# Feed-forward gate and up tiles as Strassen block products, weight-quarter sums on GpSimd (POOL)

## What is computed

```python
def swiglu_ffn(x, w_in, w_out):
    gate, up = jnp.split(x @ w_in, 2, axis=-1)
    return (jax.nn.silu(gate) * up) @ w_out

for i in range(DEPTH):                       # DEPTH = 2
    x = x + 0.5 * swiglu_ffn(rmsnorm(x, norm_g[i, 0]), ffn_w_in[i, 0], ffn_w_out[i, 0])
    ...
    x = x + 0.5 * swiglu_ffn(rmsnorm(x, norm_g[i, 2]), ffn_w_in[i, 1], ffn_w_out[i, 1])
```

## Time and profile before

| | |
|---|---|
| median of three runs | 2656.32 us |
| span of the profiled execution (the page gives no other time of it) | 2655.9 us |
| PE busy | 2612.3 us, 98% |
| DVE busy | 1569.0 us, 59% |
| ACT busy | 1004.4 us, 38% |
| POOL busy | 365.6 us, 14% |
| DMA | 238.23 MB, 90 GB/s on average |

### The profile page before, as it was taken

The page is one execution under the profiler, slowest core; times in us unless marked ns, Lnnn a source line. Parts: engine busy times, 40 slices in busy tenths (PEclk is TensorE's granted clock), DMA queues, the critical chain, the costliest instruction groups (busy, mean ns, idle before and its releaser), DMA issues.

```text
span 2655.9 us, 37310 instructions
## 1 busy us (share of the span) xinstructions
PE 2612.3 (98%) x14575; PEld 2099.3 (79%) x14575; DVE 1569.0 (59%) x2288; ACT 1004.4 (38%) x1423; POOL 365.6 (14%) x334
## 2 busy tenths in 40 slices
PE   7999999999999989999999999999999999999999
PEld 5787878787777768888888888888888864888887
DVE  6656655676767664444465444554444798644445
ACT  4544445446666642222252222232222313422223
POOL 1110101012000011111121111121111421211110
PEclk8999999999999999999999999999999999999999
DMA  3222222122222112333212223223222362233221
GB/s 117 82 80 81 80 65 95 34 80 88 79 82 78 69 53 91 98 103 99 95 64 95 96 100 101 97 94 97 95 95 95 113 170 73 97 100 101 97 95 63
DMA packets 171509, 238.23 MB, mean 90 GB/s; under 512 B 6513, under 2 KB 149371, under 8 KB 171411
## 3 DMA queue, kind: packets, MB, share of 16 engines
q1 hardware_dynamic: 163523, 217.23, 25.0%
q0 software_dynamic: 6080, 19.43, 2.6%
q10 hardware_dynamic: 1808, 0.21, 0.1%
HBM read 232.36 MB, written 4.40 MB: 89 GB/s over the span
## 4 chain that ended last, share of the span: by engine, by line
PE 88%; DVE 7%; ACT 2%; issue 1%; DMA 1%; POOL 0%; ACTq 0%; DVEq 0%; SPq 0%; POOLq 0%
PE ps L389 20%; PE ps L391 20%; PE ps L390 20%; PE ps L813 5%; PE ps L815 4%; PE ps L814 4%; DVE w_lo L366 1%; DVE dw_y L2283 1%; DVE probs L1756 1%; PE ps L375 1%; PE ps L377 1%; PE ps L376 1%; PE ps L1596 1%; PE ps L1607 1%; ACT w_hi L361 1%
## 5 line engine op out<-in xcount | busy, mean ns | idle before, releaser
L361 ACT ACTIVATE w_hi<-w_raw 128x2048 fp32r<-128x2048 f32 x203 | 388.4, 1914 | 894.8 <-PE ps L391 889.4
L389 PE MATMUL ps<-h_hi,w_hi 128*128 128x512 f32 x1456 | 569.2, 391 | 0.0
L391 PE MATMUL ps<-h_hi,w_lo 128*128 128x512 f32 x1456 | 568.0, 390 | 0.0
L390 PE MATMUL ps<-h_lo,w_hi 128*128 128x512 f32 x1456 | 567.8, 390 | 0.0
L366 DVE TENSOR_TENSOR w_lo<-w_raw,w_hi 128x2048 fp32r<-128x2048 f32 x203 | 464.9, 2290 | 126.7 <-ACT w_hi L361 126.6
L434 DVE SCALAR_TENSOR_TENSOR xT<-ps,xT 128x512 f32<-128x512 f32 x488 | 325.1, 687 | 132.5 <-PE ps L391 131.9
L389 PE MATMUL ps<-a_hi,w_hi 128*128 128x512 f32 x976 | 380.4, 390 | 2.6 <-issue 2.6
L390 PE MATMUL ps<-a_lo,w_hi 128*128 128x512 f32 x976 | 380.2, 390 | 0.0
L391 PE MATMUL ps<-a_hi,w_lo 128*128 128x512 f32 x976 | 380.2, 390 | 0.0
L1843 POOL TENSOR_TENSOR f_gate<-f_gate,n_rstd 128x512 f32<-128x512 f32 x88 | 176.8, 2011 | 1126.5 <-ACT f_gate L1837 1126.5
L389 PEld LDWEIGHTS ps<-h_hi,w_hi 128*128 128x128 f32 x1456 | 273.8, 188 | 58.1 <-issue 1.7
(11 more groups left out here) (369 smaller groups left out, 2928.5 us busy)
## 6 DMA issues: line engine op xcount, KB each, us to landing
w_raw<-in_ffn_w_in_dram SPq DMA_DIRECT2D x88, 1024.0 KB, 5.0
w_raw<-in_ffn_w_out_dram SPq DMA_DIRECT2D x44, 1024.0 KB, 4.9
w_raw<-in_a_w_in_dram SPq DMA_DIRECT2D x24, 1024.0 KB, 5.3
w_raw<-in_b_w_in_dram SPq DMA_DIRECT2D x16, 1024.0 KB, 5.4
w_raw<-in_conv_w_pw_dram SPq DMA_DIRECT2D x12, 1024.0 KB, 5.7
shifted<-glu_scratch POOLq DMA_DIRECT2D x32, 264.0 KB, 7.8
w_raw<-in_a_w_out_dram SPq DMA_DIRECT2D x8, 1024.0 KB, 4.9
w_raw<-in_b_w_out_dram SPq DMA_DIRECT2D x8, 1024.0 KB, 4.9
```

What stands on the lines that cost most here:

```text
L361: nc.scalar.activation(w_hi[:, t % 2], w_raw[:, t % 2], ACT.Copy).then_inc(hi_done, 1)
L389: nc.tensor.matmul(dst, wh, xh, start=(k == 0), stop=False)
L390: nc.tensor.matmul(dst, wh, xl, start=False, stop=False)
L391: m = nc.tensor.matmul(dst, wl, xh, start=False, stop=last)
```

## The change

In steps 2 to 10 of each feed-forward layer (`PLAIN` = 2 steps stay as they were) a gate or up tile is multiplied as 2x2 blocks: hidden channels in two halves of 128, input channels in two halves of 4 x 128, tokens in two halves of 256 (`HT`). The tile has four weight quarters of 128x512 (`corner`). Seven block products (numbered 1, 2, 5, 6, 7, 3, 4, Winograd's form) replace eight; each has 4 x 3 matmuls of 256 columns. Products add up in PSUM: 6, 7 and 4 go into the bank of 1, and 3 into that of 5, after ACT has copied what was there.

- POOL makes four sums of weight quarters per tile (`gp_step`), two of them over the raw tile. The two multiplications by `n_rstd` of such a step are gone: `n_rstd` now goes into the input blocks.
- ACT rounds (`act_mix`) and DVE subtracts (`dve_mix`) seven 128x512 parts per tile in place of one of 128x2048. They lie in `wg`, `wu` and one of the two buffers of `w_hi` and `w_lo`; the output tile of these steps has only the other one (`weight_slot`), so its rounding waits for the last output chunk of the step before (`mix_out_round`).
- Once per layer, in steps 0 and 1, DVE makes the scaled input `hs_a`, `hs_b` (8 instructions), POOL four sums of its halves (128x1024), ACT and DVE split the seven input blocks into `mix_early` and `mix_late` (`act_hs`, `dve_hs`).
- Eight small recombinations and products of 256 columns per step on DVE, five copies on ACT. In what follows g6 is product 6 of the gate tile and u6 that of the up tile; p1g, p5g, u2g (p1u, p5u, u2u) are ACT's copies of sums in PSUM, c11g, c12g, c22g (c11u, ...) DVE's recombinations of a quarter of gate or up, t2, t3, t4 POOL's input sums.
- `f_gate` moves onto `n_h`. The pooling stage's `band` now shares space with the new buffers: POOL writes it to DRAM during the attention stage and reads it back after the first feed-forward layer.
- The loops over the steps are written out.

The core of the diff (PE's products and order, POOL's sums, then the start of a steady step on ACT and DVE and the layer's start on DVE):

```diff
+            elif x in (6, 7):
+                mix_act.wait(pe, f"{'p1' if x == 6 else 'u2'}{u}", i)
+            elif x == 3:
+                mix_act.wait(pe, f"p5{u}", i)
+            elif x == 4:
+                mix_dve.wait(pe, f"c22{u}", i)
+            elif name in ("u2", "u5"):
+                mix_dve.wait(pe, "c11g" if name == "u2" else "c11u", i)
+            wh, wl = mix_slot(f, u, x)
...
+            for k in range(4):
+                ins = mm(wh, 0, first and k == 0, False)
+                mm(wh, 1, False, False)
+                ins = mm(wl, 0, False, k == 3)
+            mix_pe.done(name, ins)
 
         def pe_ff(pe, f, m, q):
...
+            for s in range(1, PLAIN):
+                for u in "guo":
+                    pe_tile(pe, step_tile(f, s, u))
+            for s in range(PLAIN, FF_STEPS):
+                for u, x in (("g", 1), ("g", 2), ("g", 5), ("g", 6), ("u", 1), ("u", 2), ("g", 7), ("u", 6), ("u", 5),
+                             ("g", 3), ("g", 4), ("u", 7)):
+                    pe_mix(pe, f, s, u, x)
+                to = step_tile(f, s, "o")
+                pe.wait_ge(lo_done, to + 1 + SPLIT_CREDIT)
+                pe.wait_ge(pair_ready, pairs_before(to) + 1)
+                pe_out(pe, to, range(0, 3))
+                pe_mix(pe, f, s, "u", 3)
+                pe_mix(pe, f, s, "u", 4)
+                pe_out(pe, to, range(3, 8))
             pe_tile(pe, t + 2 + 3 * (FF_STEPS - 1))
...
+        def gp_step(pool, f, s, u):
+
+            tt, t, i = nc.gpsimd.tensor_tensor, step_tile(f, s, u), step_at(f, s)
+            pool.wait_ge(raw_loaded[t % 2], 16 * (t // 2 + 1))
+            mix_lo_before(pool, i, u, 2)
+            tt(mix_s1, corner(t, 1, 0), corner(t, 1, 1), ALU.add).then_inc(mix_sums[u], 1)
+            mix_lo_before(pool, i, u, 3)
+            pool.wait_ge(mix_sums[u], 4 * i + 1)
+            tt(mix_s2, mix_s1, corner(t, 0, 0), ALU.subtract).then_inc(mix_sums[u], 1)
+            tt(corner(t, 1, 0), corner(t, 0, 0), corner(t, 1, 0), ALU.subtract).then_inc(mix_sums[u], 1)
+            pool.wait_ge(mix_lo[u], 6 * i + 2)
+            pool.wait_ge(mix_sums[u], 4 * i + 2)
+            tt(corner(t, 0, 1), corner(t, 0, 1), mix_s2, ALU.subtract).then_inc(mix_sums[u], 1)
+
+        def gp_ff(pool, f):
+            tt = nc.gpsimd.tensor_tensor
+            left, right = slice(0, HT), slice(HT, T)
             for c in range(2):
-                pool.wait_ge(f_silu, f_count(f, s, c, i))
-                nc.gpsimd.tensor_tensor(f_gate[:, c], f_gate[:, c], n_rstd[:], ALU.mult).then_inc(f_gated, 1)
-
-        def gp_ff(pool, f):
-            gp_gated(pool, f, 0)
-            with pool.Fori(0, FF_STEPS // 2) as i:
-                for r in range(2):
-                    gp_gated(pool, f, 1 + r, i)
-
-        def ff_round(act, f, t, i=None):
+                gp_gated(pool, f, 0, c)
+            pool.wait_ge(hs_made, 8 * f + 8)
+            tt(mix_t3[:], hs_b[:, :, right], hs_a[:, :, right], ALU.subtract).then_inc(hs_summed, 1)
+            pool.wait_ge(hs_summed, 4 * f + 1)
+            tt(hs_a[:, :, right], hs_a[:, :, right], hs_a[:, :, left], ALU.subtract).then_inc(hs_summed, 1)
+            gp_gated(pool, f, 1, 0)
+            pool.wait_ge(hs_summed, 4 * f + 2)
+            tt(mix_t2[:], hs_b[:, :, right], hs_a[:, :, right], ALU.subtract).then_inc(hs_summed, 1)
+            gp_gated(pool, f, 1, 1)
+            pool.wait_ge(hs_summed, 4 * f + 3)
+            tt(mix_t4, hs_b[:, :, left], mix_t2[:], ALU.subtract).then_inc(hs_summed, 1)
+            for s in range(PLAIN, FF_STEPS):
+                gp_step(pool, f, s, "g")
+                gp_step(pool, f, s, "u")
...
+        def act_step(act, f, s):
...
+
+            first = s == PLAIN
+            if not first:
+                mix_out_round(act, f, s)
+            pe_done("g1")
+            m("p1g", fn(f_gate[:, 0, 0:HT], half_bank(0), ACT.Copy))
+            if first:
+                weights("u", 5, 6, of=0)
+            else:
+                weights("g", 1, 2, 5)
+            pe_done("g5")
+            m("p5g", fn(f_gate[:, 1, HT:T], half_bank(3), ACT.Copy))
+            pe_done("g6")
+            m("u2g", fn(f_gate[:, 0, HT:T], half_bank(0), ACT.Copy))
+            if first:
+                weights("u", 7, of=0)
+            else:
+                weights("g", 6)
+            pe_done("u1")
...
+        def dve_step(dve, f, s):
...
+            first = s == PLAIN
+            if not first:
+                split_tile(dve, to)
+            pe_done("g2")
+            act_done("p1g")
+            m("c11g", v.tensor_tensor(gate(0, 0), half_bank(1), gate(0, 0), ALU.add))
+            if first:
+                weights("u", 5, 6, 7, of=0)
+            else:
+                weights("g", 1, 2, 5, 6)
+            pe_done("u2")
+            act_done("p1u")
+            m("c11u", v.tensor_tensor(hid(0, 0), half_bank(1), hid(0, 0), ALU.add))
+            if first:
+                weights("u", 3, 4, of=0)
...
+        def dve_ff(dve, f, m, gain, ending):
...
+            for n in range(KC):
+                into = (hs_a if n < 4 else hs_b)[:, n % 4]
+                nc.vector.scalar_tensor_tensor(into, xT[:, n], col(*gain(n)), n_rstd[:], ALU.mult, ALU.mult
+                                               ).then_inc(hs_made, 1)
...
+            u = t + 2
+            split_tile(dve, u + 1)
+            ff_scale(dve, u, 0)
+            dve_hs(dve, f, 1, 2)
+            ff_scale(dve, u, 1)
+            split_tile(dve, u + 2)
+            dve_mix(dve, f, PLAIN, "g", 1, 2)
+            dve_hs(dve, f, 5)
+            ff_product(dve, f, u, 1)
+            add = lambda *ns: add_chunks(dve, u + 2, ns, scale=0.5)
+            dve_hs(dve, f, 6)
+            add(0)
+            dve_hs(dve, f, 7)
+            add(1)
+            dve_hs(dve, f, 3)
+            add(2)
+            dve_hs(dve, f, 4)
+            add(3)
```

411 lines of the change are left out of this document (338 added, 73 removed).

## The result

The changed kernel takes **2671.06 us** (median; 2667.7 to 2671.66), the kernel before in the same comparison 2656.29 us: ratio 1.0052, 95% interval 1.0039 to 1.0064. It is slower by 14.8 us, where 16 us less were forecast. One of the five executions was a slow one (9811.08 us at a clock of 0.24); it is outside the range and the ratio, and the median of the four fast ones is 2670.4 us, 14.1 above before. The profiled execution took 2671.06 us with a span of 2669.4, so 13.5 above the span of before. The forecast range ended at 2668.

A forecast was written before the change was run, and what follows sets the result against it. TensorE was taken to bound the kernel, busy 98% of the span. Saving 58.7 us and losing 42 on entering Strassen gave -16.7 against 2655.9, 2639, forecast as 2640 us; range 2603 to 2668.

The forecast's parts named there:

- TensorE's saving, 58.7 us: Gate and up tiles: 168 matmuls at 119.8 ns replace 96 at 226.7, saving 1.63 us in each of 9 x 4 steps.
- Up-tile split 1.4 late: Layer entry, step 1: POOL's input differences hold DVE, so the up tile's split ends at 1763.7, 1.4 us late.
- 4.7 late: Layer entry: DVE's add of output chunk 0 ends at 1784.8, so TensorE's chunk 4 starts 4.7 us late.
- lands 11 us into: Second Strassen step: late gate load makes ACT, standing in order, delay g7's copy; g6, u2, g7, u5 lose 6.7 us together.
- Chunks 5 to 7: Layer entry: these output chunks wait 1.6 us more on DVE's input splits 7, 3 and 4.
- I take the middle, 0.80: Layer entry: DVE's loss per POOL instruction, 0.80 us, between 0.46 seen earlier and 1.15 for whole instructions waited out.
- the 0.46 of the earlier trace: DVE's low parts of h lose 21 us over 45 POOL additions, 0.46 us each, every second DVE instruction reading PSUM.
- the forecast's own formula: Layer entry: (price per POOL instruction - 0.27) / (1.15 - 0.27) x 17.5; at 0.80, 10.5 us a layer, 42 in all.
- the full-exclusion account, 17.5: Layer entry, POOL between any two two-SBUF-input DVE instructions: 7.7 + 3.1 + 6.7 = 17.5 us a layer.
- I add nothing: Clock after an entry stall: 4.7 us could bring 1.2 GHz once or twice a layer; no cost added, kept for range.
- The stalls stay small: Rival: entry stalls up to 5 us a layer, closely spaced DVE instructions keeping POOL out; 2598 to 2618 us, chance 0.25.
- Slower in every step: Rival: strided POOL sums of 1.7 us or more delay u5, about 2672, or 256-column pairs slow; both together 0.11.

The follow-up runs named there:

- e1: The changed kernel with POOL's weight-quarter sums cut to 8 of each 128 columns, products 5 and 6 taking plain quarters: 2626.23 us, ratio 0.9888.
- e9: The changed kernel with input sums and the first three Strassen steps' weight sums on DVE, work reordered by TensorE's need: 2654.43 us, ratio 0.9996.
- e10: Same order of work as e9, input sums on DVE, but all weight sums on POOL: 2668.04 us, ratio 1.0048.
- e6: The changed kernel with all weight sums and the four input sums per layer on DVE: 2669.66 us, ratio 1.0051.
- e2: The changed kernel with the four input sums per layer on DVE, weight sums left on POOL: 2660.84 us, ratio 1.0017.
- e3: The changed kernel with ACT's copies p5g and u2g ahead of the roundings awaiting the late load, second Strassen step: 2673.31 us, ratio 1.0063.
- e12: The kernel before, TensorE held once per feed-forward layer while POOL fills a scratch tile one, three, five, eight times: 2673.28 us, ratio 1.0064.
- e11: e9 with p1g, p5g, u2g ahead of the input-dependent roundings and DVE's late inputs behind c11g: 2635.93 us, ratio 0.9918.
- e13: e11 with, in the second Strassen step, p1g before the output tile's rounding and c11g before the previous step's last two adds: 2632.15 us, ratio 0.9910.
- e7: The changed kernel with each layer's first Strassen step's weight sums and the four input sums on DVE: 2659.32 us, ratio 1.0015.

## Why the prediction was wrong

- **TensorE's saving, 58.7 us: right.** Steps of 31.00 us, 119.8 ns a matmul. Nothing is lost in a steady step: right, with DVE at 25.7 us in it.
- **The places and their mechanism: right.** "Up-tile split 1.4 late" is the wait for L393, 1.2 in each layer; chunk 4, "4.7 late", waited 4.02 in the third layer; the load that "lands 11 us into" the second Strassen step landed at 11.7, and "ACT, which stands in order" held g7 for 3.63. Chunks 5 to 7 did not wait 1.6 for DVE; what they lose is clock.
- **The step that failed first is the weighting "I take the middle, 0.80".** One POOL instruction costs DVE 1.13 us in the entry. Of the two patterns, the 0.46 of the earlier trace rows has an instruction that reads PSUM between two that contend; the stretch from 1763 to 1791 has 10 with two SBUF inputs and 7 that read PSUM, mostly in groups, and the pair at 1732.25 in the earlier trace rows was the nearer pattern. That this difference makes the price is argued and not shown. Waiting is 14.6 us a layer, 58.5 in all, where the forecast had 10.5 and 42. The right price alone would have overshot: with 1.13 the forecast's own formula gives 17.1 us a layer, 68.4 in all, because the full-exclusion account, 17.5, is 3 too high (its chunks 5 to 7 are 1.6 of them). The two errors partly cancel.
- **The second is "I add nothing"** for clock after a stop. It is 3.8 us a layer, 15.3 in all. The row for it was at hand; the reason given, that a DVE which is behind would catch up, says nothing about the clock.
- Together: -58.7 + 58.5 + 15.3 = +15.1 against the forecast's -16.7 (14.8 by the medians, 13.5 by the spans). Each error alone would have left the result at or below no change: 16.5 us more waiting gives -0.2, the clock alone -1.4.
- **The rivals.** "Slower or even by full exclusion in the entry", 2659 to 2668 at 0.22, is what happened, 3 us beyond its end: less waiting than it said, and the clock it left out. "The stalls stay small" leant on POOL being kept out by closely spaced DVE instructions; the rows at 1764.39 and 1780.95 show the opposite. "Slower in every step" did not come: POOL's sums do average up to 2.03 us (L1977), past the 1.7 named there, but the slack of the steady step took it.

Shown by runs: the weight sums' exclusion (e1; e9 against e10; 1069 to 687 ns in e6), the input sums' (e2), the late load with copies behind it (e3 moved the wait from g7 to the next copy; in e9, with all three copies ahead, it is gone, though among other moves), the clock after a stop (e12). Not run: the order of e11 or e13 with the weight sums left on POOL. So the gain of e13 belongs to order and engine together; what the mended order alone is worth to the change as it was made stays open.

## What to carry to other kernels

POOL is no free helper beside a DVE that is behind: where DVE's instructions have two SBUF inputs, price each of POOL's at a whole instruction waited out (here 1.13 us), and look for it where a stage *starts*, not in the steady step, where slack hides it. Count the entry's work engine by engine against TensorE's deadlines, and put first on every in-order queue what TensorE waits for, above all PSUM copies of 0.4 us that can end up behind a rounding or a load; with that, and the sums of the first three Strassen steps on DVE, the same change goes from 14.8 us slower to 24.2 us faster (0.9910). Give the clock after a stop of TensorE a term of its own: here it took 15.3 us beside 58.5 of waiting.

## What the hardware showed beyond expectation

- Two DVE instructions that directly follow each other do not keep POOL out: in both pairs shown POOL ran between them, and both engines pay (DVE 4.60 us for a pair of 1.29, POOL 3.39 for one of 2.42).
- The cost in clock did not grow with the stop. TensorE worked 5.6 us at the 1.2 GHz level behind e12's stop of 3.25 us and 2.8 behind that of 5.00; behind the stops of 9.5 to 10.1 us of e9 and e10 the level lasted 3.1 to 6.0 us more.
- Which stops bring half clock, counted over all traces of this case, behind the copies of `n_rstd` (half clock during the stop or starting within 4 us behind it): 35 of 35 stops of 3.22 us or more, 10 of 12 from 3.00 to 3.21, 20 of 26 from 2.0 to 3.0. A stop of 2.03 us had it (the change, first layer), one of 2.09 (e12) and one of 3.21 (e7, fourth layer) had not. What else decides there was not separated.
